# Retention with the values of all heads first, sixteen pairs as seven products, and each output projection one head late

## Chip, core and metric

The kernel runs on one core of one Trainium2 chip. The metric is device time of one execution in microseconds (us). The core has a matrix engine (TensorE, shown as PE, with its weight loads as PEld), a vector engine (VectorE, DVE), a scalar engine (ScalarE, ACT), GpSimd (POOL) and SyncE (SP). SP and ACT both issue DMAs; each has a queue of its own in the profile (q1 for SP, q10 for ACT).

## What is computed

The reference is a transformer block with a recurrent and attention mixer, followed by two blocks on 512 latent tokens and 256 context tokens of width 1024. The change touches the retention mixer of the second part only, cut here to what it does:

```python
def retention_mixer(a_ctx, a_lat, w_in, decay_param, w_out, want_ctx):
    q, k, v, g = jnp.split(a @ w_in, [hk, 2 * hk, 2 * hk + hv], axis=-1)   # 4 heads, dk 256, dv 512
    q, k = apply_rope(q, *rope), apply_rope(k, *rope)
    ...
    o_ctx, o_lat = bidirectional_scan(ctx_terms, lat_terms)
    def readout(o, g):
        y = rms_norm_2(o)...
        return (jax.nn.silu(g) * y) @ w_out
```

The kernel computes the scan as attention with a table of decays: for each head, scores (keys by queries, 768 tokens), times a table that depends on the distance of two tokens and on the head, times the values; then a norm over the 512 outputs, times silu of the gate, times the output weights.

## The kernel before

Everything is in f32 split in a high and a low part, so each product of 128x128 weights is three matmuls (lines 2232 to 2234). The function `schedule` writes a list of items, and that list is PE's order for the main products. `Plan.arrange` draws from it the order of the other engines: each operation gets a cost and a due time, and an engine takes the ready operation that is due first. An order so drawn is then fixed, and every engine runs its own list strictly in turn with semaphore waits. In the plan a DMA issued by ACT costs 100 ns of ACT and lands 3.4 us later plus 1.3 ns for each element over 1024 of a partition, whatever else is on its way; only DMAs issued by SP are put behind one another.

`seven_pair` computes two blocks of 128 output columns for 768 tokens as seven products of half size in place of eight (P1, P5, P6, P3, P7, P2, P4), each four steps of three matmuls of 384 columns. It needs sums of token halves (T1 to T4), which DVE and ACT make once (`token_sums`, `last_sums`). A plain projection is `columns`: for one block, eight steps of three matmuls at 512 columns and the same at 256.

Retention before goes so:

- `v_rows(0)`: values of head 0 (six groups of 128 tokens by 512, 24 matmuls each), stored to DRAM by two DMAs of ACT. Then `early_gate(3, 2)`, one plain gate block, and the token sums beside them.
- 15 pairs by `seven_pair`: eight for queries and keys, seven for gates. Queries and keys of heads 1 to 3 and all gates are stored to DRAM by ACT's queue.
- for each head h: `attend(h)`, `v_rows(h + 1)`, output projection of h (`ret_o`, 96 matmuls of 512 columns and 96 of 256). For head 3 no values are left, and a plain gate block (`late_gate(3, 3)`) stands before and after the last attend's end.

`attend(h)` on PE is eight score items (`ret_score`) and eight value items (`ret_value`) in a fixed order: four scores first, of which the fourth uses bank 4 again and waits until DVE has emptied the first. The last score is followed by three value items. DVE empties a score into memory times the decay table (`ret_score`, L3558), ACT copies out the high part (L2873), DVE makes the low part (L3563). After the last value item ACT copies the four output banks (`ret_copy`, L2885) and squares them (L2890); finish, reciprocal, gating (L3586, L3592) and the split for the output projection (L2877, L3597) follow.

The decay table exists once (columns RST of the shared memory). `dist_load(h + 1)` (ACT's queue, L2810, 768 KB) waits until DVE has used the table for the last score of head h. Then `ret_decay` makes the new one: three DVE operations (L3483, L3486, L3489), three exponentials on ACT (L2802, L2804, L2806), one addition on DVE (L3495). The first score of head h + 1 cannot be emptied before.

Loads before: `v_load` for head 0 (four DMAs on ACT's queue), `qk_load` and `g_load` for each head on SP's queue, each behind its waits there.

Of the kernel before, what the change touches and what calls it, by code (L numbers as in the profile page):

```python
# [69 lines left out]
RVV, RVL, ROL, ROC, RGL, RGC, RPA, RST = 0, 3072, 6144, 8192, 9216, 11264, 12288, 13312  # L70
# [347 lines left out]
def schedule(known=()):  # L418
# [19 lines left out]
    def from_bank(i):  # L438
        turn[bank6] = i
# [254 lines left out]
    def rows_by_group(srcs, ver, after, key, dest, order=(4, 5, 0, 1, 2, 3), pairs=False, banks=(), early=0, low_dest=None, aside=False):  # L694
# [5 lines left out]
        for i in range(0, 6, size):  # L700
# [18 lines left out]
            for g in late:  # L719
                put("rows_split" if low_dest else "rows_copy", g=g.id, bank=g.bank, after=after, key=(key, g.tt), dst=dest(g.tt),  # L720
                    low=low_dest and low_dest(g.tt), aside=aside)
# [646 lines left out]
    def retention():  # L1368
# [5 lines left out]
        keys = {512: (4, 5), 0: (0, 1, 2, 3, 4, 5)}  # L1374
        ov, t, sides, staged, stores = {}, {}, [[], [], [], []], {}, {h: [] for h in range(n_head)}

        def v_rows(h):
            from_bank(4)
            rows([("ret_v", h, blk) for blk in range(4)], 4, ov["v"], ("ret_v", h), lambda tt: RVV + tt * 512, pairs=h == 0,
                 low_dest=lambda tt: (4096 if h == 0 else RVL) + tt * 512, aside=h == 0)  # L1380
# [5 lines left out]

        def early_gate(h, c):
            def post(g):
                off, after, keys_ = tmp("a", g.n)
                half = 2 + g.t0 // 512  # L1390
                put("g_plain", h=h, c=c, half=half, g=g.id, bank=g.bank, t0=g.t0, n=g.n, off=off, after=after)
                gate_store(h, c, half, g.t0, g.n, off, keys_, f"d_gp{off // 256}")
            columns([(("ret_g", h * 4 + c), (SLOT,), DC, ("h", 4), [(0, "drain_act", post)])], SEG2)

        def late_gate(h, c, after):
            def post(g):
                put("g_late", h=h, c=c, g=g.id, bank=g.bank, t0=g.t0, n=g.n, after=after)
            columns([(("ret_g", h * 4 + c), (SLOT,), DC, ("h", 4), [(0, "drain_act", post)])], SEG2[::-1])
# [77 lines left out]
        def attend(h):  # L1476

            lows = []
            for what, t0, i in order:
# [19 lines left out]
                if (t0, i) == (0, 1):  # L1499
                    finish(h, 512, 256)  # L1500
                    gated_values(h, 512, 256, range(4 if h < n_head - 1 else 3))
            if h == n_head - 1:
# [2376 lines left out]
```

## Time and profile before

| what | value |
|---|---|
| median of three runs | 2769.79 us (2769.33 to 2770.24) |
| the profiled execution | 2770.4 us, span 2768.6 us |
| PE busy | 2733.4 us, 99% |
| DVE busy | 2013.9 us, 73% |
| ACT busy | 1290.1 us, 47% |
| granted TensorE clock | 0.999 of full speed |

The span is the time from the first to the last instruction; the 1.8 us around it belong to the execution. Retention takes the stretch from about 890 to 1545 us. A row of the timeline gives start, duration, engine, line and operation, and in brackets the idle time ahead of it with what ended it. Matmuls overlap, so their cost is the distance of two starts, not the duration shown.

### The profile page before, as it was taken

To read this page: it belongs to the slowest core of one execution; us is meant where nothing else is said; L and a number is where in the kernel's file an instruction comes from. 1 tells how busy PE (TensorE), PEld (TensorE's weight loads), DVE (VectorE), ACT (ScalarE), POOL (GpSimd) and SP (SyncE) were. 2 spreads that over 40 slices of the span, in tenths; PEclk is the share of its full clock that TensorE was granted. 3 is DMA by queue.
4 is the path that set the end of the run, shared out by engine and by line. 5 is a ranking of instruction groups with operands and counts; after the bars stand their busy time and mean duration, and the time that the engine had idled before them with its cause. 6 is when DMAs were issued, how large, how long until landed. Compare 5 with 4: busy or idle time off the path is not lost.

```text
span 2768.6 us, 42922 instructions
## 1 busy us (share of the span) xinstructions
PE 2733.4 (99%) x16374; PEld 2452.4 (89%) x16374; DVE 2013.9 (73%) x3722; ACT 1290.1 (47%) x2380; POOL 372.8 (13%) x207
## 2 busy tenths in 40 slices
PE   9999999999999999999999999999999999999998
PEld 8888896988888899988888999999997787989898
DVE  7788778868896888865555996667685536778686
ACT  6332358642333645553243744344355546545354
POOL 2343300022433000011101000000002323000000
PEclk9999999999999999999999999999999999999999
DMA  6655512236654154333322022222223121222322
GB/s 204 193 186 190 168 64 84 77 110 210 191 189 152 52 206 153 126 129 141 128 75 78 25 64 74 77 65 65 76 77 96 50 81 51 75 85 92 107 92 84
DMA packets 98206, 307.48 MB, mean 111 GB/s; under 512 B 10192, under 2 KB 25424, under 8 KB 96464
## 3 DMA queue, kind: packets, MB, share of 16 engines
q1 hardware_dynamic: 90368, 279.42, 31.3%
q10 hardware_dynamic: 7632, 25.30, 2.3%
q8 instruction: 130, 2.13, 0.3%
q14 instruction: 76, 0.62, 0.1%
HBM read 282.53 MB, written 20.58 MB: 109 GB/s over the span
## 4 chain that ended last, share of the span: by engine, by line
PE 60%; DVE 6%; issue 2%; DMA 1%; ACT 1%; POOL 1%; ACTq 0%; DVEq 0%; SPq 0%; POOLq 0%
PE ps L2232 19%; PE ps L2233 18%; PE ps L2234 18%; DVE t_wlo L2977 1%; PE ps L2515 1%; PE ps L2499 1%; PE ps L2488 1%; DMA t_raw<-in_gu 1%; ACT t_whi L2558 1%; DVE t_m L3228 0%; POOL t_wlo L3677 0%; DVE t_mw L3075 0%; DVE t_m L3050 0%; DVE t_hid L3563 0%; DVE t_m L3297 0%
## 5 line engine op out<-in xcount | busy, mean ns | idle before, releaser
L2558 ACT CAST t_whi<-t_raw 128x512 fp32r<-128x512 f32 (+3 forms) x494 | 381.5, 783 | 592.2 <-PE ps L2234 391.6
L2232 PE MATMUL ps<-t_h,t_whi 128*128 128x256 f32 (+2 forms) x1852 | 624.1, 337 | 7.1 <-DVE t_wlo L2968 1.9
L2233 PE MATMUL ps<-t_h,t_wlo 128*128 128x256 f32 (+2 forms) x1852 | 619.4, 334 | 0.0
L2234 PE MATMUL ps<-t_h,t_whi 128*128 128x256 f32 (+2 forms) x1852 | 619.3, 334 | 0.0
L2977 DVE TENSOR_TENSOR t_wlo<-t_raw,t_whi 128x512 fp32r<-128x512 f32 (+3 forms) x420 | 355.3, 857 | 105.1 <-ACT t_whi L2558 101.3
L2232 PEld LDWEIGHTS ps<-t_h,t_whi 128*128 128x128 f32 x1852 | 350.3, 189 | 41.8 <-issue 10.6
L2233 PEld LDWEIGHTS ps<-t_h,t_wlo 128*128 128x128 f32 x1852 | 350.5, 189 | 26.4 <-issue 0.5
L2234 PEld LDWEIGHTS ps<-t_h,t_whi 128*128 128x128 f32 x1852 | 350.4, 189 | 26.0
L2232 PE MATMUL ps<-t_hid,t_whi 128*128 128x256 f32 (+2 forms) x1032 | 335.5, 325 | 0.6 <-DVE t_hid L3276 0.6
L2233 PE MATMUL ps<-t_hid,t_wlo 128*128 128x256 f32 (+2 forms) x1032 | 333.6, 323 | 0.0
L2234 PE MATMUL ps<-t_hid,t_whi 128*128 128x256 f32 (+2 forms) x1032 | 333.1, 323 | 0.0
L3228 DVE CUSTOM_DVE_ANT_0 t_m<-t_raw,t_m 128x1024 f32<-128x1024 f32 x192 | 298.7, 1592 | 40.8 <-DMA t_raw<-in_ada 35.5
L3677 POOL TENSOR_TENSOR t_wlo<-t_raw,t_whi 128x1024 fp32r<-128x1024 f32 (+1 forms) x74 | 182.7, 2469 | 935.2 <-ACT t_whi L2558 935.2
L2232 PE MATMUL ps<-t_mw,t_whi 128*128 128x256 f32 (+2 forms) x922 | 294.4, 319 | 4.4 <-DVE t_mw L3056 1.4
L2233 PE MATMUL ps<-t_mw,t_wlo 128*128 128x256 f32 (+2 forms) x922 | 293.2, 318 | 0.0
L2234 PE MATMUL ps<-t_mw,t_whi 128*128 128x256 f32 (+2 forms) x922 | 293.1, 318 | 0.0
L2232 PEld LDWEIGHTS ps<-t_hid,t_whi 128*128 128x128 f32 x1032 | 196.2, 190 | 16.6 <-issue 0.9
L2234 PEld LDWEIGHTS ps<-t_hid,t_whi 128*128 128x128 f32 x1032 | 196.0, 190 | 14.7
L2233 PEld LDWEIGHTS ps<-t_hid,t_wlo 128*128 128x128 f32 x1032 | 196.2, 190 | 14.5
L2232 PEld LDWEIGHTS ps<-t_mw,t_whi 128*128 128x128 f32 x922 | 174.7, 189 | 10.5 <-issue 3.9
L2233 PEld LDWEIGHTS ps<-t_mw,t_wlo 128*128 128x128 f32 x922 | 174.8, 190 | 4.0
L2234 PEld LDWEIGHTS ps<-t_mw,t_whi 128*128 128x128 f32 x922 | 174.6, 189 | 3.8
(375 smaller groups left out, 4939.6 us busy)
## 6 DMA issues: line engine op xcount, KB each, us to landing
t_raw<-in_gu SPq DMA_DIRECT2D x174, 512.0 KB, 3.4
t_raw<-in_ada SPq DMA_DIRECT2D x96, 512.0 KB, 3.8
t_raw<-in_dn SPq DMA_DIRECT2D x52, 512.0 KB, 4.1
t_raw<-in_dn SPq DMA_DIRECT2D x24, 384.0 KB, 3.4
s_qk<-t_hid ACTq DMA_DIRECT2D x12, 768.0 KB, 5.7
t_hid<-s_qk SPq DMA_DIRECT2D x6, 1536.0 KB, 11.4
t_raw<-in_ret_v SPq DMA_DIRECT2D x16, 512.0 KB, 5.2
t_raw<-in_ret_g SPq DMA_DIRECT2D x16, 512.0 KB, 3.8
```

The source lines that it names most:

```text
L2232: e.matmul(out, whi, xlo, start=first, stop=False, skip_group_check=shared)
L2233: e.matmul(out, wlo, xhi, start=False, stop=False, skip_group_check=shared)
L2234: return e.matmul(out, whi, xhi, start=False, stop=last, skip_group_check=shared)
L2488: done = e.matmul(m.PS[:, hd, :].rearrange("p (a t) -> p a t", a=2), m.na_q(qpart, it.c, it.b * P, P)[pp], m.na_keys(kpart, it.c, BAND0[it ...
L2499: done = e.transpose(m.PS[:, 2 + hd, kt * P:(kt + 1) * P], s[:, kt * P:(kt + 1) * P], m.ident)
L2515: done = e.matmul(m.PS[hd * 64:hd * 64 + 64, 4 + hd, it.b * P:(it.b + 1) * P], m.at(v, 64), m.na_t(it.to[hd])[:, kt // 2, kt % 2 * P:(kt % ...
L2558: e.copy(m.block(0, it.slot, n), m.raw(it)).then_inc(*S["hi"].of(j))
L2977: e.tensor_tensor(m.block(1, it.slot, n), m.raw(it), m.block(0, it.slot, n), ALU.subtract).then_inc(*S["lo_dve"].of(j))
L3228: e.tensor_tensor_reduce(m.at(ADA_OUT + who * 1024, 1024), m.RAW[:, it.raw % NR, :], m.cond(who), 1.0, 0.0, ALU.mult, ALU.add, m.mod(it.la ...
L3677: e.tensor_tensor(m.block(1, it.slot, n), m.raw(it), m.block(0, it.slot, n), ALU.subtract).then_inc(*S["lo_pool"].of(j))
```

## The change

- `v_rows` runs for all four heads at the start, two groups at a time, each group stored to DRAM as one DMA on ACT's queue (`v_store`, 24 of 512 KB) through a ring of eight places. `v_load` fetches each head's six blocks again by six DMAs on ACT's queue, each when the value item of the head before that used the place is done.
- All sixteen pairs go through `seven_pair`; `early_gate` and `late_gate` are gone.
- Outputs, gates and the third place for scores exist twice (h % 2). The output projection of head h comes after `attend(h + 1)`; the order on PE is attend 0, attend 1, out 0, attend 2, out 1, attend 3, out 2, out 3. Queries and keys of head 1 get a place of their own and are loaded before attend 0.
- `qk_load` and `g_load` move from SP's queue to ACT's and become items of ACT's list. The decay table and `dist_load` stay as they are.

```diff
-        early_gate(n_head - 1, 2)
+        for h in range(1, n_head):
+            v_rows(h)
         wide_slots(384)
-        gate_pairs = [(1, 0), (1, 1), (2, 0), (2, 1), (3, 0), (0, 0), (0, 1)]
...
-            if k != 3:
-                last = seven_pair("g", *gate_pairs[k - (k > 3)])
+            last = seven_pair("g", h, w)
...
-        last_h = [("ps", last["P4"])]
-        put("v_load", after=[("ps", last["P6"])])
-        put("g_load", h=0, after=last_h + stores[0])
+        tokens_read, sums_read = [("ps", last["P2"])], [("ps", last["P4"])]
+        values_back(0, lambda tt: tokens_read)
+        put("qk_load", h=1, after=tokens_read + [*kept[1]])
+        for h in range(2):
+            put("g_load", h=h, after=sums_read + stores[h])
         for h in range(n_head):
+            ov["oc"] = free_set[h % 2]
             attend(h)
             if h < n_head - 1:
                 put("dist_load", h=h + 1, after=[("drain_dve", ("ret_p", h, 0, 5))])
                 put("ret_decay", h=h + 1, after=[("p_lo", (h, 0, 5))])
-            ov["v"] = [("ret_ps", ("v", h, 0, 5, 3))]
-            if h < n_head - 1:
-                v_rows(h + 1)
-                put("qk_load", h=h + 1, after=[("ret_ps", ("s", h, 0, 5))] + [staged[w] for w in range(2)])
+                values_back(h + 1, lambda tt, h=h: [("ret_ps", ("v", h, 0, keys[0].index(tt), 3))])
+                if h != 1:
+                    put("qk_load", h=max(h + 1, 2), after=[("ret_ps", ("s", h, 0, 5)), *kept[max(h + 1, 2)]])
...
+            if h:
+                done = output(h - 1)
+                free_set[(h - 1) % 2] = [done]
+                if h + 1 < n_head:
+                    put("g_load", h=h + 1, after=[done] + stores[h + 1])
...
+    def v_store(it):
+        w.wait_ge("drain_act", (("ret_v", it.h), it.tt))
+        w.wait_ge("drain_dve", (("ret_v", it.h), it.tt))
+        e.dma_start(dram["s_v"][it.h][:, it.tt * 1024:it.tt * 1024 + 1024], m.HID[:, it.at * 1024:it.at * 1024 + 1024].bitcast(F32))...
+
     def v_load(it):
+        w.wait_ge(f"d_vs{it.at}", (it.h, it.tt))
         wait_all(it.after)
-        w.wait_ge("d_vs0", 0)
+        e.dma_start(m.H[:, it.tt * 1024:it.tt * 1024 + 1024].bitcast(F32), dram["s_v"][it.h][:, it.tt * 1024:it.tt * 1024 + 1024])...
+
+    def qk_load(it):
+        wait_all(it.after)
...
+    def g_load(it):
+        wait_all(it.after)
+        e.dma_start(m.at(it.h % 2 * RSET + RGATE, 3072).rearrange("p (c t) -> p c t", c=4), dram["s_g"][it.h])...
```

## Rows read from the trace of the kernel before

**Rows 1.** The page, busy time, share and instructions of each engine.
```profile
PE 2733.4 (99%) x16374; PEld 2452.4 (89%) x16374; DVE 2013.9 (73%) x3722; ACT 1290.1 (47%) x2380; POOL 372.8 (13%) x207
```

**Rows 2.** Windows: stretch, length, busy (instructions) of PE, PEld, DVE, ACT, POOL, clock, DMA.
```profile
950.00:1000.00 50.00, 45.53 (x255) 42.55 (x253) 45.70 (x88) 24.99 (x49) 0.00 (x0) 1.00 0.39 143
...
1200.00:1250.00 50.00, 50.00 (x221) 41.02 (x220) 30.70 (x46) 23.21 (x34) 3.69 (x2) 1.00 0.12 42
```

**Rows 3.** Windows of 4 us at the first pairs, same columns.
```profile
960.00:964.00 4.00, 2.72 (x16) 2.40 (x16) 3.86 (x8) 3.12 (x7) 0.00 (x0) 1.00 0.05 16
...
968.00:972.00 4.00, 2.49 (x13) 2.04 (x12) 3.86 (x9) 0.75 (x2) 0.00 (x0) 1.00 0.40 131
972.00:976.00 4.00, 3.28 (x16) 2.67 (x17) 4.00 (x9) 0.00 (x0) 0.00 (x0) 1.00 0.38 131
```

**Rows 4.** Timeline of PE, two waits in that stretch.
```profile
972.07 0.44 PE L2232 MATMUL ps<-t_mw,t_whi 128*128 128x384 f32 x1 [1.37 <-DVE t_mw L3056]
...
975.38 0.41 PE L2232 MATMUL ps<-t_h,t_whi 128*128 128x384 f32 x1 [0.51 <-DVE t_hid L3549]
```

**Rows 5.** Timeline of PE, distances of matmuls: 384, 512 and 256 columns.
```profile
1182.42 0.33 PE L2234 MATMUL ps<-t_mw,t_whi 128*128 128x384 f32 x1
1182.59 0.39 PE L2232 MATMUL ps<-t_hid 128*128 128x512 f32 x1
1182.82 0.40 PE L2233 MATMUL ps<-t_hid 128*128 128x512 f32 x1
...
1188.14 0.28 PE L2234 MATMUL ps<-t_hid,t_mw 128*128 128x256 f32 x1
1188.26 0.28 PE L2232 MATMUL ps<-t_hid,t_mw 128*128 128x256 f32 x1
```

**Rows 6.** Timeline of PE: after the last score of head 0; first value row of head 1.
```profile
1204.89 0.39 PE L2232 MATMUL ps<-t_hid,t_mw 128*128 128x512 f32 x1
...
1213.05 0.39 PE L2232 MATMUL ps<-t_wlo,t_h 128*128 128x512 f32 x1
```

**Rows 7.** Timeline of DVE, the table's last use and its remaking for head 1.
```profile
1205.09 0.69 DVE L3558 SCALAR_TENSOR_TENSOR t_m<-ps,t_m 128x512 f32<-128x512 f32 x1 [0.41 <-PE ps L2234]
...
1210.07 0.69 DVE L3483 TENSOR_SCALAR t_m<-t_m,t_tmp 128x896 f32<-128x896 f32 x1 [1.55 <-DMA t_m<-in_dist]
...
1211.51 1.09 DVE L3489 TENSOR_TENSOR t_m<-t_m 128x896 f32<-128x896 f32 x1
...
1219.90 0.82 DVE L3495 TENSOR_TENSOR t_m<-t_m 128x640 f32<-128x640 f32 x1 [1.38 <-ACT t_m L2806]
```

**Rows 8.** Timeline of ACT over the same stretch.
```profile
1205.82 0.34 ACTq L2810 DMA_DIRECT2D t_m<-in_dist  x1
...
1211.21 2.63 ACT L2885 COPY t_m<-ps 128x512 f32<-128x512 f32 x4 [4.20 <-PE ps L2234]
...
1215.94 1.28 ACT L2802 ACT_TABLE_LOAD   x1
1217.24 0.95 ACT L2802 ACTIVATE t_m<-t_m 128x896 f32<-128x896 f32 x1
...
1219.04 0.83 ACT L2806 ACTIVATE t_m<-t_m,t_tmp 128x640 f32<-128x640 f32 x1
```

**Rows 9.** ACT's DMAs, L2820, the last two v_loads, issued at 1175.3 and 1175.9.
```profile
DMA to landing us min/median/max: 11.0/12.4/13.9
```

**Rows 10.** ACT's DMAs, line L2868, the gate store issued at 1178.9.
```profile
DMA to landing us min/median/max: 12.0/12.0/12.0
```

**Rows 11.** ACT's DMAs, line L2810, the four loads for the decay table.
```profile
DMA to landing us min/median/max: 4.2/4.3/4.4
```

**Rows 12.** Windows with the v_loads under way, then all of attend 0; columns as above.
```profile
1176.00:1180.00 4.00, 4.00 (x25) 4.00 (x25) 3.19 (x5) 2.25 (x3) 1.43 (x1) 1.00 1.01 367
1180.00:1184.00 4.00, 4.00 (x23) 3.73 (x23) 1.57 (x3) 3.96 (x5) 1.01 (x1) 1.00 1.03 423
...
1182.60:1213.10 30.50, 29.92 (x148) 24.92 (x148) 21.61 (x36) 16.80 (x32) 3.15 (x2) 1.00 0.57 215
```

More of the change, by code:

```diff
@@ L692, in rows, with rows_by_group @@
             pass
-    def rows_by_group(srcs, ver, after, key, dest, order=(4, 5, 0, 1, 2, 3), pairs=False, banks=(), early=0, low_dest=None, aside=False):
+    def rows_by_group(srcs, ver, after, key, dest, order=(4, 5, 0, 1, 2, 3), pairs=False, banks=(), early=0, low_dest=None, done=None):
         held = [block(s, (SLOT,)) for s in srcs]
@@ L719, in rows_by_group @@
             for g in late:
-                put("rows_split" if low_dest else "rows_copy", g=g.id, bank=g.bank, after=after, key=(key, g.tt), dst=dest(g.tt),
-                    low=low_dest and low_dest(g.tt), aside=aside)
+                put("rows_split" if low_dest else "rows_copy", g=g.id, bank=g.bank, after=after(g.tt) if done else after, key=(key, g.tt), dst=dest(g.tt),
+                    low=low_dest and low_dest(g.tt))
+                if done:
+                    done(g)
             late = []
@@ L1373, in retention, with v_store @@
         score_bank = {(0, 0): 4, (512, 0): 5, (512, 1): 7, (0, 1): 4, (0, 2): 5, (0, 3): 4, (0, 4): 5, (0, 5): 4}
[L1374 to L1375 removed]
+        keys = {512: (4, 5), 0: (4, 5, 0, 1, 2, 3)}
+        ov, t, sides, staged, kept, stores = {}, {}, [[], [], [], []], {}, {}, {h: [] for h in range(n_head)}
         def v_rows(h):
             from_bank(4)
[L1379 to L1380 removed]
+            ring = lambda tt: (h * 6 + (4, 5, 0, 1, 2, 3).index(tt)) % 8
+            rows([("ret_v", h, blk) for blk in range(4)], 4, lambda tt: [(f"d_vs{ring(tt)}", ov["ring"][ring(tt)])] if ring(tt) in ov["ring"] else state["hid_free"],
+                 ("ret_v", h), lambda tt: ring(tt) * 1024, pairs=True, low_dest=lambda tt: ring(tt) * 1024 + 512,
+                 done=lambda g: v_store(h, g.tt, ring(g.tt)))
+        def v_store(h, tt, at):
+            put("v_store", h=h, tt=tt, at=at)
+            ov["ring"][at] = (h, tt)
         def gate_store(h, c, half, t0, n, off, keys_, name):
@@ L1572, in retention @@
-            if h == n_head - 1:
-                for slot in (9, 10):
-                    give(slot, ov["v"])
-            if h < n_head - 1:
-                from_bank(4)
-            done = columns([(("ret_o", j2, h), (2, 512), 4, ("yr", h), outs(j2)) for j2 in range(4)],
-                           SUB2 if h == 3 else SEG2, batch=4 if h == 3 else 1)
-            ov["oc"] = [done]
-            ov["p"][2] = ov["p"][2] + ov["oc"]
-            if h < n_head - 1:
-                put("g_load", h=h + 1, after=[done] + stores[h + 1])
+                state["hid_free"] = state["h_free"] = [("ret_ps", ("v", h, 0, 5, 3))]
@@ L2445, in ret_score @@
             if it.h:
[L2446 removed]
+                w.wait_ge(f"d_qk{it.h}", "all")
             else:
@@ L2845, in qk_store @@
                 *S[f"d_qs{it.w}"].of((it.h, part), it.h))
-    def g_plain(it):
-        w.wait_ge("ps", it.g)
-        wait_all(it.after)
-        e.activation(m.tmp(it.off, it.n), m.PS[:, it.bank, 0:it.n], ACT.Silu).then_inc(*S["drain_act"].of(it.g, ("g", it.h, it.c, it.half)))
     def g_last(it):
@@ L2855, in g_last @@
         e.activation(m.tmp(it.off, it.n), m.PS[:, it.bank, 0:it.n], ACT.Silu).then_inc(*S["drain_act"].of(it.key, ("g", it.h, it.c, it.half)))
-    def g_late(it):
-        w.wait_ge("ps", it.g)
-        wait_all(it.after)
-        e.activation(m.ret_gate(it.c, it.t0, it.n), m.PS[:, it.bank, 0:it.n], ACT.Silu).then_inc(*S["drain_act"].of(it.g, ("g_late", it.t0)))
     def g_silu(it):
```

174 lines of the change are left out of this document (76 added, 98 removed).

## The prediction

> **What bounds the kernel now.** I read the page first. PE is busy 99% of the span [rows 1], so two things can move the time: the number of PE's cycles, and the few places where PE stands still. The granted clock is 1.00 in all windows read here [rows 2, 3], which is the 2.4 GHz level, so the clock plays no part. I then cut retention into windows of 50 us. The stretch 950 to 1000 holds 4.47 us of idle PE with DVE busy for 45.70 of 50 us, while 1200 to 1250, the end of head 0 with the values of head 1 behind it, holds none [rows 2]. Windows of 4 us place most of the idle time at the first pairs: 1.28, 1.51 and 0.72 us, in all 3.51 us, and DVE is busy for nearly all of those 12 us [rows 3]. The timeline of PE names the releasers: a low part of a token sum on DVE, and the drain of a value group that DVE reached late [rows 4]. So PE outran DVE there because only 33 us of values and one gate block stood ahead of the pairs. Last I read where a head hands over to the next, since that is what the new order changes [rows 6 to 8], and how ACT's queue behaves under load [rows 9 to 12].
>
> **The change part by part.**
>
> *Gates.* Two plain blocks go: 2 blocks x 8 steps x 3 = 48 matmuls at 512 columns and 48 at 256. Starts lie 0.23 and 0.12 us apart (0.226 where many are counted: 50 us over 221 matmuls, mostly of 512 columns [rows 2, 5]), so 48 x 0.226 + 48 x 0.120 = 16.6 us. One seven-product pair comes: 7 x 4 x 3 = 84 matmuls at 0.173 [rows 5] = 14.5 us. Gain 2.1 us. The matmuls for values, scores and outputs stay the same in number.
>
> *Values first.* Values of heads 1 to 3 are 3 x 144 x 0.226 = 98 us of PE work now ahead of the first pair. DVE has one 0.69 us operation for each group of 5.4 us there, so the token sums are done long before. The 3.51 us go, all of them. The rest of that window, 4.47 - 3.51 = 0.96 us, is idle time of pairs that run on; I take half of it, 0.5, between 0 and 1. The 24 stores cost ACT an issue of some 0.34 us each, the duration of the row for line 2810 [rows 8], and hide behind PE, since ACT is idle for over half of that time [rows 1]. The weight blocks come at the same rate as in the separate stages before.
>
> *Head 0 to head 1.* This decides. The table is remade between the last drained score of a head and the first drained score of the next. In the kernel before, 65 us of values and output projection cover it. In the new order the same holds for the hand-overs to heads 2 and 3, with 33 us of output projection, but between attend 0 and attend 1 nothing stands. PE can run the rest of attend 0, until 1213.05 [rows 6], and three scores of head 1, 6 x 0.226 + 12 x 0.120 = 2.8 us; then the fourth needs bank 4. So PE is at a stop at 1215.9 on the clock of the old trace. What must be ready by then:
>
> - the load, issued at 1205.82 and used by DVE from 1210.07, 4.3 us later [rows 7, 8, 11];
> - three DVE operations until 1211.51 + 1.09 = 1212.6, 2.5 us [rows 7];
> - the exponentials, 1217.24 to 1219.87, 2.6 us [rows 8];
> - the addition 0.8 us, the drain of the first score 0.7 us [rows 7], some 0.2 us of signals. After landing this is 2.5 + 2.6 + 0.8 + 0.7 + 0.2 = 6.8 us.
>
> With an undisturbed load the table would land at 1210.1; ACT is held by the output copies until 1213.84 and a table load of 1.28 us [rows 8], so the exponentials end at 1217.8 and PE goes on at 1219.4. That is a stop of 3.5 us even at its best order (if the exponentials went ahead of the copies, about 1 us, the lower bound).
>
> *ACT's queue.* The load isn't undisturbed. A gate store of 192 KB issued at 1178.9, behind the four v_loads, landed after 12.0 us [rows 10], at 1190.9, just after the last of them (1175.9 + 13.9 = 1189.8) [rows 9]. So ACT's queue works through its transfers in order. The rate is 367 to 423 GB/s in the first two windows of [rows 12], 0.40 MB per us for both queues together. From the end of P2 at 1180.5 (1182.59 less 12 x 0.173) the new kernel puts on this one queue: values of head 0, 3.15 MB; queries and keys of head 1, 3.15; the last gate stores, 0.6; gates of heads 0 and 1, 3.15; three value blocks of head 1, 1.57. That is 11.6 MB, and about 1.0 MB of weights on SP's queue share the engines. At 0.40 this takes 31.5 us, to 1212. Then comes either the table's load, 0.79 MB, or ahead of it the queries and keys of head 2, 3.15 MB. Those are released by PE's last score at about 1204.9, the table's load only by the drain of that score, 0.9 us later at 1205.8 [rows 6, 7]. ACT stood idle between the two, and its list takes what is ready. So I expect the 3.15 MB ahead: 12.6 + 3.15 + 0.79 = 16.5 MB, 41.3 us, to 1222, and with some 2 us from the last byte's issue to the signal (4.3 us less 2.0 us of transfer [rows 11]) the table's load lands at 1224. Plus 6.8 us: PE goes on at 1231, a stop of 15.0 us.
>
> The Trainium skill ("DMA: Bandwidth & Descriptors", section "Queues, rings and completion order") says that each DMA engine takes one ring's descriptors in order and goes round between the rings by packets; by that rule loads left on SP's queue would have shared with the table's load instead of standing ahead of it, so moving them speaks against this change. The 12.0 us store agrees with the first half, and the sum would be the same by it.
>
> *DVE in attend 1.* The tail of head 0 (a reciprocal of 512 columns, and twelve operations of that size for gating and splits, each 0.69 us as in [rows 7], 8.3 us) falls beside attend 1. An attend keeps DVE busy for 21.6 of 30.5 us by itself [rows 12]. That is about full. I take 1 us, between 0 and 4; the long stop gives DVE time for it.
>
> *The rest.* At the end, output 2 covers the tail of head 3 as the late gate did. I take 0.
>
> Sum: -2.1 - 3.5 - 0.5 + 15.0 + 1.0 = +9.9 us on the profiled 2770.4, so 2780.3; the median lies 0.6 us lower, and I forecast 2780 us.
>
> **The rivals.**
>
> *A, the table's load goes ahead of the queries and keys of head 2.* It lands at 1216, PE goes on at 1223, a stop of 7 us. Sum -6.1 + 7 + 1 = +1.9: 2772. For it: the load is due much sooner. Against: it is ready 0.9 us later.
>
> *B, the queue is clear by then*, because gate loads come late or transfers run faster. The stop is 3.5 us, the sum -1.6: 2768. By the Trainium skill ("ScalarE: Activation LUTs", "What ACT_TABLE_LOAD costs") a switch of tables is about 2.7 us with its drain, and this stop would be 1.4 us longer; the row shows 1.28 us and the next activation 0.02 us behind it.
>
> *C, faster: the hand-over is hidden.* One mechanism: the table for head 1 is ready when PE has done its third score. It decides if the last addition ends by 1215.2, which asks for a landing near 1209 with the exponentials ahead of the copies. Then the gains stand alone: -6.1, 2764. Against: 4.3 us of transfer alone bring it to 1210.
>
> *D, ACT is blocked earlier as well.* The load of the gates now stands in ACT's own list and waits for the last gate stores, which lie behind 3.15 to 6.3 MB: landing from 1193 to 1202. If ACT gets there at 1192, the copies of score parts behind that wait are late and PE stops 2 to 5 us in attend 0. On top of the forecast that is up to 5 us, of which a part is given back at the hand-over, since the queue works on; I take 4: 2784.
>
> **How the numbers follow.** The forecast 0.48, A 0.18, B 0.10, C 0.16, D 0.08. A measurement here can tell 0.2%, 5.5 us, from no change: forecast and D are slower, 0.56; A and B the same, 0.28; C is faster, 0.16. The forecast's own range is 2774 to 2785 (rate 0.37 to 0.42, DVE 0 to 4). To hold 8 in 10 the range takes in A, B and most of C, 2763, and at the top D's 2785 with DVE's upper bound of 4 in place of 1, 2788, one more for rounding, 2789.
>
> **What would show it.** After: no idle PE of over 0.5 us at the first pairs, and 84 matmuls of 384 columns more; one long wait of PE in the first 3 us of attend 1, ended by the drain of a score, whose own wait is for the addition of the table, and behind it a DMA that took far over 4.3 us. The issues on ACT tell forecast from A. If PE waits inside attend 0 for an ACT copy whose engine stood at a DMA's semaphore, it is D. The prediction is wrong if ACT's transfers overtake each other, or if I have the order of ACT's list wrong.

## The result: 2795.7 us, slower, and by more than the range held

The changed kernel takes 2795.68 us (median of 5 runs, 2794.72 to 2798.67) against 2769.79 of the kernel before on the same chip: a ratio of 1.0097, 95% interval 1.0082 to 1.0111. I had forecast 2780 and a range of 2763 to 2789. The direction was right; the size was +25.9 us where I had +9.9.

In the changed kernel the names of the lines are these: L2463 is the product that sums the squares of a head's output (a "mean product"), L2223 the first of three products, L2873 ACT's squares, L3558 DVE's sum of them, L3541 DVE's drain of a score (the table's use), L3466 to L3478 DVE's part of the table, L2790 ACT's exponentials, L2798 the table's load, L2820 the load of rotated queries and keys ("tokens" below), L2851 a gate store.

The page of the changed kernel, busy times:

```profile
span 2792.9 us, 43013 instructions
PE 2734.7 (98%) x16362; PEld 2457.0 (88%) x16362; DVE 2030.1 (73%) x3735; ACT 1287.6 (46%) x2384; POOL 367.9 (13%) x206
```

PE is busy 1.3 us more than in [rows 1], in a span that is 24.3 us longer. So most of the loss is time in which it stands still. The waits of PE, by what ended them (total, times, longest):

```profile
PE ps L2463 <- DVE t_tmp L3558: 23.2, 3, 13.2
PE ps L2223 <- DVE t_m L3541: 10.2, 1, 10.2
PE ps L2258 <- DMA t_par<-in_params: 3.0, 1, 3.0
```

These first two rows, 33.4 us in four waits, aren't in the trace of before. The timeline of PE places them (start, duration, in brackets the idle time ahead and who ended it):

```profile
1303.43 1.19 PE L2463 MATMUL ps<-t_tmp,t_con 128*128 128x256 f32 x2 [13.20 <-DVE t_tmp L3558]
...
1336.63 0.80 PE L2223 MATMUL ps<-t_h 128*128 128x512 f32 x1 [10.15 <-DVE t_m L3541]
...
1368.10 0.67 PE L2463 MATMUL ps<-t_tmp,t_con 128*128 128x256 f32 x2 [1.37 <-DVE t_tmp L3558]
...
1449.68 2.07 PE L2463 MATMUL ps<-t_tmp,t_con 128*128 128x512 f32 x2 [8.65 <-DVE t_tmp L3558]
```

I call the three long ones stop 1 (inside attend 0), stop 2 (between attend 0 and attend 1) and stop 3 (behind attend 2, where output 1 was meant to be the cover). Stop 2 is the one that I had forecast. The windows around stop 1 show more than the wait (columns as in [rows 2]):

```profile
1292.00:1296.00 4.00, 0.00 (x0) 0.00 (x0) 0.00 (x0) 0.00 (x0) 0.00 (x0) 0.72 0.98 385
1296.00:1300.00 4.00, 0.00 (x0) 0.00 (x0) 0.00 (x0) 0.00 (x0) 0.00 (x0) 0.50 0.77 285
1300.00:1304.00 4.00, 0.57 (x2) 0.51 (x3) 2.21 (x4) 3.41 (x6) 0.72 (x1) 0.50 0.57 173
1304.00:1308.00 4.00, 4.00 (x12) 3.15 (x11) 1.23 (x3) 0.95 (x3) 0.00 (x0) 0.58 1.02 430
1308.00:1312.00 4.00, 4.00 (x20) 3.29 (x19) 3.72 (x6) 0.97 (x2) 0.00 (x0) 1.00 0.95 373
```

For 8 us no engine is busy, and DMA runs at 285 to 385 GB/s: everybody waits for a transfer. And the granted clock falls to 0.50, the 1.2 GHz level, so that PE does 12 matmuls in the first 4 us after the stop and 20 in the next. It does so behind stop 2 too:

```profile
1336.00:1340.00 4.00, 3.37 (x10) 2.79 (x11) 3.00 (x7) 3.18 (x7) 0.51 (x1) 0.50 0.19 77
1340.00:1344.00 4.00, 4.00 (x26) 3.87 (x26) 2.52 (x4) 2.07 (x5) 0.77 (x1) 0.81 0.01 2
```

An estimate of what that costs is PE's busy time in such a window times the part of the clock that is missing: 0.57 x 0.50 + 4.00 x 0.42 = 2.0 us behind stop 1, 3.37 x 0.50 + 4.00 x 0.19 = 2.4 behind stop 2, and 2.2 behind stop 3 (its windows stand further down), 6.6 us in all.

What they wait for is in ACT's timeline at stop 1:

```profile
1281.53 0.33 ACTq L2820 DMA_DIRECT2D t_h<-s_qk  x1
1281.89 0.46 ACTq L2820 DMA_DIRECT2D t_h<-s_qk  x1
...
1283.93 1.33 ACTq L2851 DMA_DIRECT2D s_g<-t_tmp  x3
...
1300.57 0.42 ACT L2873 ACTIVATE t_tmp<-t_m 128x256 f32<-128x256 f32 x1 [12.29 <-DMA s_g<-t_tmp]
```

ACT's squares need temporary slots that still hold gates; the last gate stores of head 0 were issued 2 us behind the tokens of head 1, 3.15 MB, and the values of head 0. They take 15.7 us to land, and ACT stands for them, and DVE behind ACT. At stop 2, ACT and then DVE:

```profile
1315.56 0.81 ACTq L2820 DMA_DIRECT2D t_hid<-s_qk  x2
1316.41 0.44 ACTq L2798 DMA_DIRECT2D t_m<-in_dist  x1
...
1332.27 0.95 ACT L2790 ACTIVATE t_m<-t_m 128x896 f32<-128x896 f32 x1 [8.02 <-DVE t_m L3472]
```

```profile
1329.70 0.69 DVE L3466 TENSOR_SCALAR t_m<-t_m,t_tmp 128x896 f32<-128x896 f32 x1 [11.46 <-DMA t_m<-in_dist]
...
1334.92 0.83 DVE L3478 TENSOR_TENSOR t_m<-t_m 128x640 f32<-128x640 f32 x1 [1.38 <-ACT t_m L2794]
```

The order is the one that I had expected: tokens of head 2 first, the table's load 0.85 us behind. It lands after 13.3 us against 4.3 [rows 11], and from there to PE's first matmul it is 1336.63 - 1329.70 = 6.9 us. Stop 3 has the same pair of issues (1423.56 tokens, 1424.95 table); that load took 13.2 us. ACT stands 7.1 us at the exponentials, and its squares of attend 2, which are behind them in its list, begin at 1443.26. The trace also has the same load without tokens ahead of it: the table of head 2, issued at 1358.65, landed after 6.4 us, and PE waited only the 1.4 us at 1368.10.

**A ledger by phases.** From the first pair's stretch on, values and pairs took 268.5 us before (914.1 to 1182.6) and 365.9 now (912.4 to 1278.3). Now they hold 98 us of values and a pair of 14.5 more, and the early gate block of 8.3 less, so 268.5 + 104.2 - 365.9 = 6.8 us were won. Attends and outputs took 367.9 us and now 298.8, with 98 + 8.3 = 106.3 us of work taken out: 37.2 us lost. Of these 33.4 are waits. The other 3.8 are the slower clock, 6.6, less 2.8 us of idle time that the kernel before had there (PE is busy for 365.2 of the 368.0 us from 1182.6). The gates' 2.1 is the difference of 104.2 and 106.3. Small shifts ahead of and behind retention gave 1.7 and 2.2 us. In all 37.2 - 6.8 - 2.1 - 1.7 - 2.2 = 24.4, against 24.3 in the spans. Of the 6.8 us won, the windows show 4.7 as idle time of PE that is gone (5.5 us before, 0.8 now); the other 2.1 I can't place.

### The profile page after: what moved, and what is told of

The parts are those of the page before. It is cut to its first block, busy times and chain, and to the rows that moved or that the text cites. A ratio compares the mean times of both kernels' runs of the same rounds, so it can differ in the third digit from the quotient of the medians.

```text
span 2792.9 us, 43013 instructions
## 1 busy us (share of the span) xinstructions
PE 2734.7 (98%) x16362; PEld 2457.0 (88%) x16362; DVE 2030.1 (73%) x3735; ACT 1287.6 (46%) x2384; POOL 367.9 (13%) x206
## 4 chain that ended last, share of the span: by engine, by line
PE 61%; DVE 4%; DMA 3%; ACT 1%; issue 1%; POOL 1%; ACTq 0%; DVEq 0%; SPq 0%; POOLq 0%
PE ps L2223 19%; PE ps L2224 19%; PE ps L2225 19%; DMA t_m<-in_dist 1%; PE ps L2503 1%; PE ps L2487 1%; PE ps L2476 1%; DMA s_g<-t_tmp 1%; DVE t_wlo L2960 1%; DMA t_raw<-in_gu 1%; DVE t_m L3211 0%; ACT t_whi L2546 0%; POOL t_wlo L3658 0%; PE ps L2463 0%; DVE t_m L3280 0%
## 5 line engine op out<-in xcount | busy, mean ns | idle before, releaser
L2223 PE MATMUL ps<-t_h,t_whi 128*128 128x256 f32 (+2 forms) x1832 | 616.7, 337 | 4.5 <-DVE t_wlo L2951 1.3
L2224 PE MATMUL ps<-t_h,t_wlo 128*128 128x256 f32 (+2 forms) x1832 | 612.6, 334 | 0.0
L2225 PE MATMUL ps<-t_h,t_whi 128*128 128x256 f32 (+2 forms) x1832 | 612.5, 334 | 0.0
L2960 DVE TENSOR_TENSOR t_wlo<-t_raw,t_whi 128x512 fp32r<-128x512 f32 (+2 forms) x424 | 357.9, 853 | 110.4 <-ACT t_whi L2546 106.1
L2223 PEld LDWEIGHTS ps<-t_h,t_whi 128*128 128x128 f32 x1832 | 346.5, 189 | 37.5 <-issue 10.1
L2225 PEld LDWEIGHTS ps<-t_h,t_whi 128*128 128x128 f32 x1832 | 346.6, 189 | 25.4
L2223 PE MATMUL ps<-t_hid,t_whi 128*128 128x256 f32 (+2 forms) x1032 | 335.5, 325 | 0.7 <-DVE t_hid L3259 0.7
L2223 PE MATMUL ps<-t_mw,t_whi 128*128 128x384 f32 (+2 forms) x938 | 301.5, 321 | 0.9 <-ACT t_tmp L2551 0.8
L2224 PE MATMUL ps<-t_mw,t_wlo 128*128 128x384 f32 (+2 forms) x938 | 298.9, 319 | 0.0
L2225 PE MATMUL ps<-t_mw,t_whi 128*128 128x384 f32 (+2 forms) x938 | 298.9, 319 | 0.0
L2223 PEld LDWEIGHTS ps<-t_hid,t_whi 128*128 128x128 f32 x1032 | 196.2, 190 | 16.7 <-DVE t_hid L3259 0.9
L2223 PEld LDWEIGHTS ps<-t_mw,t_whi 128*128 128x128 f32 x938 | 178.2, 190 | 6.6 <-issue 2.6
L2225 PEld LDWEIGHTS ps<-t_mw,t_whi 128*128 128x128 f32 x938 | 178.0, 190 | 4.0
```

The lines of the kernel that those rows point to most:

```text
L2223: e.matmul(out, whi, xlo, start=first, stop=False, skip_group_check=shared)
L2224: e.matmul(out, wlo, xhi, start=False, stop=False, skip_group_check=shared)
L2225: return e.matmul(out, whi, xhi, start=False, stop=last, skip_group_check=shared)
L2960: e.tensor_tensor(m.block(1, it.slot, n), m.raw(it), m.block(0, it.slot, n), ALU.subtract).then_inc(*S["lo_dve"].of(j))
```

## The experiments

Theory: three stops, each because something small that is needed soon was issued behind something large that is needed late; and a clock that falls after each. The main rival for each stop is a chain of its own (the hand-over, DVE's load) or sheer DMA bandwidth, whatever the order. All ratios are to the kernel before, with runs of it on the same chip; its median there is 2769.8 to 2770.4 us, so medians of two experiments can be compared to within some 0.6 us beside their own spread.

### The table's load first

```
-  put("qk_load", h=max(h + 1, 2), after=[("ret_ps", ("s", h, 0, 5)), *kept[max(h + 1, 2)]])
+  put("qk_load", h=max(h + 1, 2), after=[("ret_ps", ("s", h, 0, 5)), ("ret_gs", h + 1), *kept[max(h + 1, 2)]])
```

> The changed kernel with one wait added: ACT issues the load of the rotated tokens of heads 2 and 3 only when the decay table of the next head is done, so that the 0.79 MB of the table's load goes ahead of them on ACT's queue. Theory (queue order): the table's load lands in 4 to 6 us, in place of 13.3 and over 12; the stop at the hand-over to head 1 falls from 10.2 us to 2 to 4 us, the one behind attend 2 from 8.7 us to 0 to 4 us, the first stop of 13.2 us stays as it is, and 2 to 5 us more come back where the clock no longer falls: 2780 us, from 2775 to 2785. Rival 1 (the hand-over's own chain): both stops stay over 7 us, 2790 or more. Rival (the tokens of head 2, issued some 10 us later, come late for attend 2): a new wait of PE on that load, and under 5 us of gain.

Measured: 2776.7 us, ratio 1.0025 (1.0016 to 1.0034), inside the range. One wait added takes 19.0 us away. The table's load lands in 5.6 to 6.0 us. PE's waits in this kernel:

```profile
PE ps L2463 <- DVE t_tmp L3558: 13.4, 3, 12.1
PE ps L2223 <- DVE t_m L3541: 2.4, 1, 2.4
PE ps L2223 <- DMA t_h<-s_v: 1.7, 1, 1.7
```

Stop 2 is 2.4 us, stop 3 is gone, stop 1 (12.1) stands. Queue order holds for stops 2 and 3, and their own chains are worth 2.4 and 0. In the profiled runs the span is 18.5 us shorter, though the values start 1.4 us later here (913.8 against 912.4), so retention is 19.9 us shorter. These waits are 33.4 - 17.5 = 15.9 of that; the other 4.0 go with two stretches of half clock, 2.0 each, near the 2.4 and 2.2 estimated above.

### The same loads from another queue

```
+        elif it.kind == "qk_load":
+            for ev in it.after:
+                w.wait_ge(*ev)
+            for part in range(2):
+                ...
+                e.dma_start(to.bitcast(F32), dram["s_qk"][it.h, part]).then_inc(*S[f"d_qk{it.h}"].of(part, "all"))
+        elif it.kind == "g_load":
+            ...
-    "v_load": v_load, "qk_load": qk_load, "g_load": g_load, "ret_decay": ...
+    "v_load": v_load, "ret_decay": ...
```

> The changed kernel with one part undone: the rotated tokens and the gates of the next heads are loaded from SP's queue again, as in the kernel before, and no longer from ACT's. Theory (ACT's one queue, served in order): the decay table's load, 13.3 us from issue to landing behind 3.15 MB of rotated tokens, lands in 4 to 8 us; the stops of 10.2 us (head 0 to head 1) and 8.7 us (behind attend 2) come down to at most 4 us each; the gate stores, now behind the value loads alone, cut the stop of 13.2 us to 4 to 8 us; and less time at the half clock behind each stop: 2775 us, from 2766 to 2783. Rival 1 (the chain of the hand-over itself, table remade between two heads, sets the stop): the stops of 10.2 and 8.7 us stay at 7 us or more and the time is 2788 or more. Rival 2 (DMA bandwidth, whatever the queue): the table's load still takes over 10 us, 2790 or more. Rival 3 (SP's weight loads are blocked behind the waits that SP now has): PE waits for weights on SP's queue, and the time is no better than 2795.

Measured: 2788.3 us, 1.0064 (1.005 to 1.0078), 7.4 us better than the change and 13 us short of my 2775. Stop 1 is 10.0 us, stop 2 7.3, stop 3 5.6. The landing of the table's load, issued at 1317.03:

```profile
DMA to landing us min/median/max: 10.6/10.6/10.6
```

That is between 5.6 (ahead of the tokens) and 13.3 (behind them). Theory was half right: rival 2 of this run, shared bandwidth, has most of it. (The gate stores were also issued later, from 1289.5 in place of 1283.9, and still took 10.8 to 13.2 us, with no tokens ahead of them on their own queue.) The Trainium skill ("DMA: Bandwidth & Descriptors", "Queues, rings and completion order") says that each DMA engine goes round between the rings it has work for; the trace agrees, with 10.6 us for 0.79 MB beside 3.15 MB on the other queue. I had used this rule in the prediction to say that the move of the loads "speaks against this change". It does, by 7.4 us of 26; the order is worth more than the queue.

### The gate stores first

```
-  put("qk_load", h=1, after=tokens_read + [*kept[1]])
+  put("qk_load", h=1, after=tokens_read + [*kept[1]] + stores[0])
```

> The changed kernel with one wait added: the load of head 1's rotated tokens is issued behind the last gate stores of head 0 instead of ahead of them, so that these stores stand behind the value loads alone. Theory (ACT's squares in attend 0 wait for temporary slots whose gate stores lie behind 3.15 MB of tokens on ACT's queue): the stop of 13.2 us in attend 0 falls to 4 to 7 us, the clock's fall behind it shortens, all else stays: 2787 us, from 2783 to 2790. Rival (the stop comes from ACT's own work order or from PE's early arrival, not from the stores): the stop stays at 12 us or more and the time at 2794 to 2797.

Measured: 2790.3 us, 1.0075 (1.0061 to 1.0089), just above the range. PE's waits around stops 1 and 2:

```profile
1296.17 0.67 PE L2463 MATMUL ps<-t_tmp,t_con 128*128 128x256 f32 x2 [2.11 <-DVE t_tmp L3558]
1310.92 0.50 PE L2223 MATMUL ps<-t_mw,t_h 128*128 128x512 f32 x1 [1.58 <-DVE t_mw L3546]
...
1333.67 0.80 PE L2223 MATMUL ps<-t_h 128*128 128x512 f32 x1 [12.98 <-DVE t_m L3541]
```

Stop 1 falls from 13.2 to 2.1 us, more than expected; the stores land in 5.4 to 6.6 us. But only 5.3 us reach the time: stop 2 grew from 10.2 to 13.0, and 1.6 us opened between. PE is earlier at stop 2, and the table's load stands behind the same bytes.

### The gate stores from another queue, alone and with the table first

```
+            if (h, c // 2) == (0, 1):
+                last_stores.append(it)
+            else:
+                put("g_store", **it)
...
         values_back(0, lambda tt: tokens_read)
+        for it in last_stores:
+            put("g_store_sp", **it)
```

> The changed kernel with one part altered: the last four gate stores of head 0 are issued from SP's queue, so that no load of ACT's queue lies ahead of them. Theory: ACT's squares in attend 0 find their temporary slots free, the stop of 13.2 us there falls to 0 to 4 us and the clock no longer falls behind it; the hand-over to head 1 and the stop behind attend 2 stay at 8 to 13 us: 2783 us, from 2779 to 2789. Rival 1 (the stores share the DMA engines with the value loads, so another queue does not help): a stop of 8 us or more stays, 2790 to 2795. Rival 2 (time that PE gains in attend 0 is given back at the hand-over, where the table's load stands at the same place of ACT's queue and lands when it landed before): the stop of 10.2 us grows by as much as the first one shrinks, 2790 to 2795.

> Both mends in one: the last gate stores of head 0 from SP's queue, and the decay table's load ahead of the rotated tokens of heads 2 and 3 on ACT's queue. Theory (three stops, each from ACT's queue, and the clock behind each): the run with the table's load first measured 2776.7 us with a first stop of 12.1 us left; without it 12 us and some 2 us of half clock go, up to 4 us come back at the hand-over: 2764 us, from 2759 to 2770, so faster than both kernels. Rival (the hand-over's own chain of 3.5 us and more, or DVE in attend 1, takes back what is won): 2770 to 2777.

Measured: 2791.7 us, 1.0077 (1.0062 to 1.0092), and 2772.7 us, 1.001 (1.0001 to 1.002). Neither does what I expected. SP's issue and landing in the second of them:

```profile
L2204 SPq DMA_DIRECT2D s_g<-t_tmp x4: 424/431/460, 1290.0 to 1291.4; - x4
...
DMA to landing us min/median/max: 12.2/12.8/12.8
```

SP got to them at 1290.0, 4.4 us later than ACT had issued its last ones in the run with the table first (1285.6), and beside ACT's loads they took 12.8 us. Stop 1 was 7.2 us with the stores alone moved and 6.8 in the second. That is near rival 1 of the first of the two runs: another queue did not take these small stores out of the burst. It isn't a clean test, since SP was late, and one of its own weight loads of 0.5 MB, issued at 1289.6, stood just ahead of the stores. With the stores alone moved stop 2 was 12.1 us: of the 6.0 us that stop 1 gave, stop 2 took 2.0.

### The table made early

```
             put("g_load", h=h, after=sums_read + stores[h])
+        put("dist_load", h=1, after=sums_read)
+        put("ret_decay", h=1, after=sums_read)
...
+            e.tensor_tensor(m.at(RST + 896, 640), gs, tb[:, 0:640], ALU.add).then_inc(*S["ret_gs"].of(h))
+            e.tensor_scalar(m.at(RST, 896), ll, 1.0, None, ALU.mult).then_inc(*S["ret_ll"].of(h))
```

> The changed kernel with one part altered: the decay table of head 1 is loaded and worked out before attend 0, in the output area of set 1, and only its last addition and one copy follow the last score of head 0. Theory: the stop of 10.2 us at the hand-over to head 1 was the table's load and the chain behind it, and falls to 0 to 3 us, with the clock's fall behind it; the other two stops stay: 2786 us, from 2781 to 2790. Rival 1 (DVE's work in attend 1, not the table, holds PE there): the stop stays over 6 us and the time over 2791. Rival 2 (the table's 0.79 MB and 3 us of DVE and ACT work ahead of attend 0 push back the squares of attend 0): the first stop grows by 2 us or more, 2788 to 2793.

Measured: 2928.8 us, 1.0578 (1.056 to 1.0595), a miss by 143 us. DVE and PE in it:

```profile
1302.72 0.69 DVE L3473 TENSOR_SCALAR t_m<-t_m,t_tmp 128x896 f32<-128x896 f32 x1 [15.04 <-DMA t_m<-in_dist]
```

```profile
1313.59 0.80 PE L2230 MATMUL ps<-t_hid 128*128 128x512 f32 x1 [29.93 <-DVE t_m L3554]
```

With the new item the planner put both tables' loads, head 0's too, at 1284.5 and 1285.0 on ACT's queue, behind values and tokens. In the changed kernel DVE is at head 0's table at 1271.8. Here it stood 15.0 us for the first load, with the scores of attend 0 undrained behind it: a wait of 29.9 us of PE. That is less than a quarter of the 133 us that this version loses against the changed kernel. PE is idle for 60.7 us from 1278 to 1560 (33.6 in the changed kernel) and for 63.1 us from 1700 to the end (13.4 there), far behind retention, in the new order of the work that the planner wrote around this item; I did not take those waits apart. As a test of stop 2 it says nothing. It shows one more wait behind a load that was issued late, the longest.

### Idle time filled, for the clock

```
   wait_all(it.before)
+  for _ in range({(0, 512): 46, (2, 0): 28}.get((it.h, it.t0), 0)):
+      e.matmul(m.PS[:, it.bank, 0:128], m.one512, m.ident, start=True, stop=True)
   w.wait_ge("ret_dve", ("s", it.h, it.t0))
```

> The changed kernel with idle time of PE filled: 46 extra products of 128 columns ahead of the first mean product of attend 0, and 28 ahead of the one behind attend 2; each goes to a bank that the mean product then overwrites, so nothing that is computed changes. The waits of 13.2 and 8.7 us stand there anyway. Theory (the clock falls behind a stop because PE stood idle, and that costs 2.0 to 2.4 us each): granted clock 1.00 behind both places, some 4.5 us less: 2791.5 us, from 2789.5 to 2794. Rival 1 (the fall of the clock costs nothing, since other engines set the pace there): no change, 2795 to 2797. Rival 2 (the extra products outlast the waits): slower than 2797.

Measured: 2794.5 us (2791.2 to 2796.5), 1.0086 (1.0071 to 1.0101); half a microsecond above its range; by the time it can't be told from the changed kernel. The windows show the effect on the clock at stop 3, first the changed kernel, then this one:

```profile
1448.00:1452.00 4.00, 2.32 (x4) 1.20 (x5) 2.02 (x2) 0.21 (x1) 1.07 (x1) 0.50 0.36 119
1452.00:1456.00 4.00, 4.00 (x14) 3.16 (x13) 0.95 (x2) 0.47 (x1) 0.00 (x0) 0.73 0.03 12
```

```profile
1448.00:1452.00 4.00, 1.86 (x11) 1.19 (x10) 1.88 (x4) 2.03 (x3) 1.26 (x1) 1.00 0.15 62
1452.00:1456.00 4.00, 4.00 (x21) 3.33 (x20) 3.54 (x2) 1.62 (x2) 2.13 (x1) 1.00 0.00 0
```

With the stop filled the clock stays at 1.00. From this mean product to the next head's, PE took 1487.7 - 1449.7 = 38.0 us in the changed kernel and 1487.8 - 1450.9 = 36.9 here. But the two stretches don't hold the same work. The planner chooses the place of a mean product in PE's list, and with the extra products it chose another. The matmul ahead of it in the changed kernel, then both neighbours in this one:

```profile
1440.64 0.39 PE L2225 MATMUL ps<-t_mw,t_whi 128*128 128x512 f32 x1
```

```profile
1442.38 6.41 PE L2463 MATMUL ps<-t_con 128*128 128x128 f32 x56
1450.94 1.13 PE L2465 MATMUL ps<-t_tmp,t_con 128*128 128x512 f32 x2 [2.14 <-DVE t_tmp L3560]
1451.50 0.69 PE L2223 MATMUL ps<-t_mw,t_whi 128*128 128x256 f32 x1
```

Three matmuls of 256 columns and three of 512, 3 x 0.120 + 3 x 0.226 = 1.0 us, stood ahead of it and now stand behind. So the clock had cost 1.1 + 1.0 = 2.1 us at stop 3. That agrees with the 2.2 from the windows, and with the 2.0 to 2.4 that I had expected. At stop 1 the gain did not last: PE waited 4.3 us more after the filling, and stop 2, bound to a transfer, came 3.3 us later.

### The sixteenth gate pair alone, on the kernel before

```
-  early_gate(n_head - 1, 2)
-  gate_pairs = [(1, 0), (1, 1), (2, 0), (2, 1), (3, 0), (0, 0), (0, 1)]
+  gate_pairs = [(1, 0), (1, 1), (2, 0), (2, 1), (3, 0), (3, 1), (0, 0), (0, 1)]
...
-  late_gate(h, 3, ov["oc"])
```

> The kernel before with one part of the change alone: the sixteenth pair (the third and fourth gate matrix of head 3) as seven products too, in place of one gate matrix multiplied early and one late in the plain way; everything else as before. Theory: 2.1 us less (18 products' difference, and nothing waits for it), 2767.7 us, from 2766 to 2770. Rival 1 (the late gate had filled a stop at the last head, which now opens): 2770 to 2775. Rival 2 (the pair's extra sums on DVE hold PE at the start of the pairs): 2771 to 2774.

Measured: 2777.3 us, 1.0026 (1.0016 to 1.0036): 7.1 us slower, not 2.1 faster, and above the ranges of both rivals, since both came true. Two windows (columns as before), PE's longest wait from 950 to 1000, and its waits from 1500 to 1550, where the kernel before has one of 0.9 us:

```profile
950.00:1000.00 50.00, 42.41 (x222) 39.73 (x223) 46.04 (x89) 23.95 (x46) 0.00 (x0) 0.97 0.41 150
...
1500.00:1550.00 50.00, 45.11 (x288) 40.80 (x287) 37.72 (x75) 15.83 (x29) 3.64 (x2) 0.93 0.07 22
```

```profile
PE ps L2226 <- DVE t_hid L3544: 4.1, 2, 3.6
...
PE ps L2226 <- DVE t_mw L3590: 3.1, 3, 1.7
PE ps L2469 <- DVE t_tmp L3570: 1.7, 1, 1.7
```

The early block had covered DVE at the first pairs (3.1 us more idle time than in [rows 2], 45.53 - 42.41), and the late one the tail of head 3 (49.08 - 45.11 = 4.0 us, and the clock falls to 0.93). That is 7.1 us of idle time. Windows of 2 us put some 4 us on the slower clock, by the estimate used above; 2.1 us of products are gone, and 1.3 us of idle time elsewhere in retention. The sum, some 8, is near the 7.1 measured. So the plain blocks were not waste: in the old order each filled a stop. That the extra sums of the new pair on DVE have no part in the first stop is not shown; both came with one edit. In the changed kernel values and output 2 do this work: PE is busy all the time from 1040 to 1060, where its first pair begins, and from 1500 to 1550.

### Both orders together, then what was left

The first kernel has the two waits of the first and third experiment. The second has this as well:

```
             put("g_load", h=h, after=sums_read + stores[h])
+        put("dist_load", h=1, after=sums_read)
...
+        e.dma_start(m.at(RSET if it.h == 1 else RST, 1536), dram["dist"]).then_inc(*S[f"d_dist{it.h}"].of(0))
...
+        raw = m.at(RSET, 896) if h == 1 else ll
```

> The changed kernel with only the order on ACT's queue altered, by the two waits tried singly before: the decay table's load ahead of the rotated tokens of heads 2 and 3, and the last gate stores of head 0 ahead of the rotated tokens of head 1. No stop's load or store then stands behind 3.15 MB of tokens. Theory: from the 2776.7 us of the first alone, whose one long stop was 12.1 us in attend 0; the second alone left 2.1 and 1.6 us of waits in its place. 12.1 - 3.7 = 8.4 us, and 2.4 us of half clock behind it: 2766 us, from 2761 to 2771, faster than the kernel before. Rival (as with the gate stores alone, PE's time won in attend 0 comes back at the hand-over to head 1, whose table cannot be begun before the queue has moved 6.3 MB of tokens and gates): the stop at the hand-over grows from 2.4 to 6 us or more, 2770 to 2776.

> The same order, and the distances of head 1's table loaded ahead of time into the output area of set 1, which is empty until head 1's first score is scaled; DVE and ACT make the table from there at the hand-over, when the old one is read for the last time. Theory (the hand-over's own chain was 4.3 us of landing and 6.8 us of work, of which PE's own reserve covers most): the stop of 2 to 3 us at the hand-over to head 1 goes, 2 to 4 us less than the kernel without this: 2763 us, from 2758 to 2768. Rival (the load, 0.79 MB more among the crowded loads before attend 0, pushes back the gates and squares by 2 us, and the hand-over's stop was hidden in part): within 1 us of the kernel without it.

Measured: 2773.3 us, 1.0011 (1.0002 to 1.002), and 2768.8 us, 0.9995 (0.9987 to 1.0004). The first came out at its rival's time, though the stop is 5.1 us where the rival asked for 6: PE's waits in it

```profile
1314.25 0.79 PE L2223 MATMUL ps<-t_mw,t_h 128*128 128x512 f32 x1 [3.94 <-DVE t_mw L3546]
...
1329.50 0.79 PE L2223 MATMUL ps<-t_h 128*128 128x512 f32 x1 [5.13 <-DVE t_m L3541]
```

show a hand-over of 5.1 us and a new wait of 3.9. With the distances loaded ahead of time the hand-over's wait is 0.4 us and the time 4.5 less. That is more than the 2 to 4 of the theory, and still 0.8 over its range, which was counted from a base that did not come true. The new wait stays (4.3 us), and DVE's timeline in this kernel tells what it is:

```profile
1311.06 0.42 DVE L3577 TENSOR_TENSOR t_m<-t_m 128x256 f32<-128x256 f32 x1 [8.98 <-DMA t_m<-s_g]
```

The gates of head 0 stand behind the tokens of head 1: a fourth case of the same thing. The order of these loads was changed next:

```
+        put("g_load", h=0, after=sums_read + stores[0])
         put("qk_load", h=1, after=tokens_read + [*kept[1]] + stores[0])
+        put("g_load", h=1, after=sums_read + stores[1])
```

> The last version (table ahead of tokens, stores ahead of tokens, head 1's distances ahead of time) with one order more: the gates of head 0 are loaded ahead of the rotated tokens of head 1, not behind them. In the last version DVE stood 9.0 us for these gates, which stand behind 3.15 MB of tokens, and PE 4.3 us behind it. Theory (the same mechanism a fourth time: a small load that is needed first behind a large one that is needed later): the wait of 4.3 us and 1 to 2 us of half clock behind it go, 2763 us, from 2760 to 2767, and faster than the kernel before. Rival (the burst as a whole, some 9.4 MB at about 0.42 MB/us before attend 1, is the limit, and what is put first only moves the wait to the tokens of head 1 or to its values): another wait of 3 us or more takes its place, 2767 to 2770.

and in the last one, with no step of its own for head 0's gates:

```
     def qk_load(it):
         wait_all(it.after)
+        if it.h == 1:
+            e.dma_start(m.at(RGATE, 3072).rearrange("p (c t) -> p c t", c=4), dram["s_g"][0]).then_inc(*S["d_g0"].of(0))
         for part in range(2):
```

> As the last version, but with the order that it did not bring about: there the rotated tokens of head 1 were still issued 1.0 us ahead of the gates of head 0. Here both loads are one step, the gates first. Theory: the gates, 1.57 MB, land some 7.5 us sooner, DVE's wait of 6.5 us for them goes and with it PE's 1.8 us: 2765 us, from 2762 to 2767. Rival (the burst as a whole is the limit): the tokens of head 1, 4 us later, or its values are waited for in place of the gates, and the time is 2766 to 2770.

Measured: 2767.0 us, 0.9989 (0.998 to 0.9998), and 2763.3 us, 0.9976 (0.9965 to 0.9987). The first edit did not do what it says: the tokens were still issued first, since the list is written by what is ready. What it measured can't be told from the kernel without it. The second did it; ACT's issues and DVE's wait:

```profile
1285.57 0.48 ACTq L2828 DMA_DIRECT2D t_m<-s_g  x1
...
1290.01 0.33 ACTq L2821 DMA_DIRECT2D t_m<-s_g  x1
1290.37 0.94 ACTq L2824 DMA_DIRECT2D t_h<-s_qk  x2
```

```profile
1301.77 0.43 DVE L3578 TENSOR_TENSOR t_m<-t_m 128x256 f32<-128x256 f32 x1 [1.40 <-DMA t_m<-s_g]
```

The first of these rows shows one more difference: it is the load of head 1's gates, another 1.57 MB. It now goes ahead of the tokens too, and had stood behind them in the version before (1293.00 against 1291.59). DVE waits 1.4 us where it had waited 9.0 and 6.5, and PE's longest wait in retention is 2.0 us. This version is faster than both kernels: 6.5 us less than the one before, 32.4 less than the change as it was made. Its runs spread from 2759.7 to 2767.5, so the last step alone is not settled to a microsecond.

## Why the prediction was right or wrong

*Gates*, -2.1: the number of products holds; the ledger uses the same prices (104.2 - 106.3) and so can't test them. Where it stands in the kernel matters more than I wrote: alone it costs 7.1 us.

*Values first*, -3.5 and -0.5: right. PE's idle time in this part went from 5.5 to 0.8 us. By the ledger 6.8 us came back, not 4.0; 2.1 of them are not seen as idle time and stay open.

*Head 0 to head 1*: right for this hand-over. I gave 6.8 us from landing to PE and 3.5 at best; the trace shows 6.9, and the stop was 2.4 to 5.1 us where the tokens were held back.

*ACT's queue*, +15.0: mechanism and order of issue right. The stop was 10.2, because stop 1, which I had not counted, gave the queue 13.2 us to work on. Without stop 1 (gate stores first) it was 13.0, near the forecast.

*DVE in attend 1*, +1.0: no wait of this kind is seen; 0. The 8.3 us of DVE work in its sum leave out the reciprocal, 3.35 us in the trace (1348.16, L3563), and with it 21.6 + 8.3 + 3.4 = 33.3 us of DVE work stand against 30.5 us of attend 1. That nothing came of it may be luck: stop 2 gave DVE time.

**The steps that failed** are three terms that the forecast put at nothing.

The first is stop 1, 13.2 us. In *ACT's queue* the last gate stores of head 0 are only 0.6 MB on the way to the table's load; the sum has nobody waiting for them. Rival D, "ACT is blocked earlier as well", had the place right (attend 0, ACT at a DMA's semaphore, gate stores behind tokens), with a chance of 0.08 and 2 to 5 us. But it let ACT wait at the gates' load, and only copies of score parts be late. In the trace ACT waits earlier, for the temporary slots under those stores, and its squares are late.

The second is stop 3, 8.7 us, and the wait of 1.4: *The rest*, 0, with the sentence in *Head 0 to head 1* that "in the new order the same holds for the hand-overs to heads 2 and 3, with 33 us of output projection". I asked only whether PE has work until the table is ready. I did not ask what else is in ACT's list behind the exponentials: the squares of attend 2, for which PE waits at a mean product placed inside the cover. The wait of 1.4 at 1368 is the same thing in DVE's list, where the sum for a mean product (1367.53) stands behind the table's three operations. The load of head 3's tokens ahead of that table's load follows from the same order as at stop 2, and I priced it at nothing.

The third is that "the clock plays no part", which was true of before only. Behind each long stop PE ran at 0.50 for 4 to 5 us. That cost 2.0 to 2.4 us a stop by the windows, 2.1 at stop 3 by the filled stop and 2.0 each by the run with the table first: 6.6 us for three.

By terms: -2.1 - 6.8 + 33.4 of waits + 6.6 of clock - 2.8 of idle time that attends and outputs had before = 28.3, less 3.9 of shifts outside retention: 24.4, against 24.3 of span. The forecast's +9.9 lacked 23.2 us (stops 1 and 3 and the wait of 1.4) and 6.6 of clock. It had 4.8 too much for stop 2, 1.0 for DVE, 2.8 too little gain at the pairs, and none of the 2.8 and the 3.9: 9.9 + 29.8 - 15.3 = 24.4. So the errors in the other direction hid half of what was left out, and that the range was missed by only 7 us is luck.

Shown by runs: the order of ACT's transfers makes stops 2 and 3 (table first), stop 1 (stores first), and the wait for head 0's gates (forced order); a second queue helps little. Argued only: that stop 1 is what made stop 2 shorter than forecast (it grew from 10.2 to 13.0 when stop 1 went, but the rate of the transfers was not varied), and where 2.1 us of the gain at the pairs come from. The last step, from 2767.0 to 2763.3, moved head 1's gates too.

## What to carry to other kernels

When loads are moved onto one queue (as here, where each engine works its list strictly in turn), write the list of all transfers of that stretch with their bytes, and for each the first instruction that needs it, stores included: a store's landing frees a slot, and the engine that wants the slot is stopped as by a load. Issue by need, not by readiness; here three such orders and one early load are worth 32 us, and the loads on a second queue 7. When PE seems covered, follow each in-order list past the stalled instruction to the next one that PE waits for. Price the slower clock behind each long stop too. And work that looks like the slow form may be somebody's cover: price it by what stands idle without it.

## What the runs showed of the hardware

The table's load of 0.79 MB took 4.3 us alone [rows 11], 5.6 to 6.0 with the tokens held back, 10.6 with 3.15 MB of them on another queue, and 13.3 behind them on its own. And PE's granted clock fell from 1.00 to 0.50 in each stop of 6.8 us or more whose windows I read. It once fell behind a wait of only 2.0 us, with 0.8 us idle 11 us before, in the last run but one:

```profile
1296.00:1300.00 4.00, 4.00 (x12) 3.19 (x11) 3.31 (x4) 1.64 (x3) 0.00 (x0) 0.60 1.01 417
```

In the last run such waits are 2.0 and 0.9 us long, 9 us apart, and the clock stays at 1.00 behind them. So these runs don't show what decides it. The Trainium skill ("TensorE: Matmul & The Clock Gate", "What's actually happening") lets this clock depend on how busy PE has been of late; the filled stop, where the clock held 1.00, agrees.
